# Memory's keys by 512-column products, and eight taps of a convolution moved to GpSimd, in a two-layer hybrid decoder

## What is computed

```python
z = rms_norm(x, mix_norm[l]) @ w_in[l]          # attention q, k, v; convolution; short convolution
ca, cg = jnp.split(zc, 2, axis=-1)
u = ca * jax.nn.sigmoid(cg)                     # 256 channels
u = causal_depthwise_conv(u, cc_dw[l]) + cc_dw_b[l]   # 31 taps for each channel
o_cc = jax.nn.silu(layer_norm(u, cc_ln_g[l], cc_ln_b[l]))
x = x + jnp.concatenate([o_att, o_cc, o_sc], axis=-1) @ w_out[l]
hq = (rms_norm(x, xa_norm[l]) @ xa_wq[l])       # cross attention, 4 heads of 256
kv = rms_norm(mem, mem_norm[l]) @ xa_wkv[l]     # 256 memory tokens: mk (keys), mv (values)
```

## Time and profile before

| | us |
|---|---|
| median of 3 runs | 1152.06 (1151.82 to 1153.53) |
| the profiled execution's own time | 1151.6 |
| its span in the trace | 1149.8 |
| granted TensorE clock | 0.999 of full |
| busy: PE, DVE, ACT, POOL | 1142.5, 845.7, 655.3, 24.0 |
| HBM traffic | 183 GB/s over the span |

### The profile page before, as it was taken

How to read it: one execution, slowest core, us unless ns; L and a number is a source line. 1 busy time by engine, 2 the same in 40 slices (tenths; PEclk the granted TensorE clock), 3 DMA queues, 4 the chain that set the end, 5 groups by cost and what they waited for, 6 DMA issues and landing times.

```text
span 1149.8 us, 15912 instructions
## 1 busy us (share of the span) xinstructions
PE 1142.5 (99%) x6316; PEld 993.5 (86%) x6316; DVE 845.7 (74%) x1152; ACT 655.3 (57%) x937; POOL 24.0 (2%) x63
## 2 busy tenths in 40 slices
PE   9999999999999999999999999999999999999997
PEld 8888888889889888888888888888898898888886
DVE  7767667899867676666776676669998676766756
ACT  6555656547755564545565554564577556645444
POOL 1000000001000000000000000000010000000000
PEclk9999999999999999999999999999999999999999
DMA  8965645643444366555546655544445443656551
GB/s 283 317 205 173 208 156 177 220 164 134 181 161 168 111 225 200 185 187 198 188 152 247 202 182 192 193 160 172 181 147 201 165 147 124 224 172 210 172 191 62
DMA packets 58970, 210.93 MB, mean 183 GB/s; under 512 B 4880, under 2 KB 15888, under 8 KB 52752
## 3 DMA queue, kind: packets, MB, share of 16 engines
q1 hardware_dynamic: 57920, 209.26, 53.7%
q10 hardware_dynamic: 976, 0.66, 0.2%
HBM read 208.85 MB, written 1.05 MB: 183 GB/s over the span
## 4 chain that ended last, share of the span: by engine, by line
PE 99%; DVE 0%; DVEq 0%; ACT 0%; issue 0%
PE G L1659 28%; PE G L1663 15%; PE D L1511 10%; PE D L1512 10%; PE D L1513 10%; PE G L1511 4%; PE G L1513 4%; PE G L1512 3%; PE G L1620 3%; PE G L1626 1%; PE D L1620 1%; PE D L1594 1%; PE D L1540 1%; PE D L1542 1%; PE D L1541 1%; PE G L1540 1%
## 5 line engine op out<-in xcount | busy, mean ns | idle before, releaser
L962 DVE TENSOR_TENSOR w_lo<-w_raw,w_hi 128x2048 fp32r<-128x2048 f32 (+3 forms) x260 | 452.5, 1747 | 58.4 <-ACT w_hi L556 57.2
L556 ACT ACTIVATE w_hi<-w_raw 128x2048 fp32r<-128x2048 f32 (+3 forms) x260 | 381.9, 1478 | 42.1 <-PE G L1513 18.4
L1659 PE MATMUL G<-a,w_hi 128*128 128x512 f32 x1406 | 339.8, 390 | 0.0
L1659 PEld LDWEIGHTS G<-a,w_hi 128*128 128x128 f32 x1406 | 260.8, 188 | 52.7 <-issue 0.9
L1663 PEld LDWEIGHTS G<-a,w_lo 128*128 128x128 f32 x1406 | 184.2, 191 | 9.5
L1663 PE MATMUL G<-a,w_lo 128*128 128x256 f32 x1406 | 187.0, 282 | 0.0
L1066 DVE TENSOR_TENSOR zqk<-G,zqk 128x512 f32<-128x512 f32 x88 | 60.8, 691 | 153.1 <-ACT zqk L635 152.8
L635 ACT ACTIVATE zqk<-G 128x512 f32<-128x512 f32 x88 | 52.5, 596 | 180.2 <-PE G L1663 180.0
L1511 PE MATMUL D<-w_hi,hT_hi 128*128 128x512 f32 x352 | 138.2, 393 | 0.0
L1512 PE MATMUL D<-w_lo,hT_hi 128*128 128x512 f32 x352 | 137.9, 392 | 0.0
L1513 PE MATMUL D<-w_hi,hT_lo 128*128 128x512 f32 x352 | 137.0, 389 | 0.0
(11 more groups left out here) (261 smaller groups left out, 1366.5 us busy)
## 6 DMA issues: line engine op xcount, KB each, us to landing
w_raw<-w_dram SPq DMA_DIRECT2D x128, 1024.0 KB, 5.1
w_raw<-w_dram SPq DMA_DIRECT2D x127, 512.0 KB, 5.5
m_raw<-memT_dram SPq DMA_DIRECT2D x2, 1024.0 KB, 10.1
w_raw<-w_dram SPq DMA_DIRECT2D x6, 256.0 KB, 5.6
w_raw<-w_dram SPq DMA_DIRECT2D x8, 128.0 KB, 3.8
vx<-mem_dram SPq DMA_DIRECT2D x1, 1024.0 KB, 11.8
x<-x_dram SPq DMA_DIRECT2D x2, 256.0 KB, 5.0
gbc<-fin_dram SPq DMA_DIRECT2D x1, 512.0 KB, 8.0
```

Of the source, the lines that this page charges most:

```text
L556: A(w_hi[:, part(i)], w_raw[:, part(i)], ACT.Copy).then_inc(s_hi, 1)
L962: V.tensor_tensor(w_lo[:, part(i)], w_raw[:, part(i)], w_hi[:, part(i)].bitcast(F32), ALU.subtract).then_inc(s_lo, 1)
L1659: M(banks[b], whi[:, at:at + P], both, start=k == 0, stop=False)
```

## The change

Blocks kv 0 to kv 3 are cut as 8 row groups of 256 columns and come in two transfers each. The memory's hi and lo are put in one tensor m, and `tall` is gone: the keys go through `head_queries` (renamed `head_columns`), 16 products of 512 columns and 16 of 256 for each block, with blocks alternating between DB[2:4] and G[0:2]. ACT and DVE make the keys' high and low parts after each of the four blocks, so TensorE waits for kvlo0 before kv 2, kvlo1 before kv 3, kvlo2 before kv 4, kvlo3 before kv 6, and for max1 already before kv 1. Taps 23 to 30 leave DVE; POOL computes them into acc3 (which is the tensor sig) as soon as u_pad is there, and DVE adds acc3 after acc2. The orders of ACT and DVE in the stretch kv 2 to kv 5 are rewritten.

```diff
+    name[1] == "kv" and name[2] < 4) else 1 for name, _ in RING_BLOCKS]
...
-        m_hi = sb("m_hi", [P, KD, T], F32R)
-        m_lo = sb("m_lo", [P, KD, T], F32R)
+        m = sb("m", [P, KD, 2, T], F32R)
+        m_hi, m_lo = m[:, :, 0, :], m[:, :, 1, :]
...
+        DVE_TAPS = 23
+        K_BANKS = (DD[:, 2:4, :], GG[:, 0:2, :])
...
+                pool.wait_ge(conv_act.sem, conv_act.at(l, "uT"))
+                for j in range(DVE_TAPS, KC):
+                    to = acc3 if j == DVE_TAPS else tap
+                    for c in range(2):
+                        last = nc.gpsimd.tensor_scalar(to[:, c, :], u_pad[:, c, j:j + T], col(C_CCW + c * KC + j), None,
+                                                       ALU.mult)
+                    if j > DVE_TAPS:
+                        pool.drain()
+                        last = nc.gpsimd.tensor_tensor(acc3[:, :, :], acc3[:, :, :], tap[:, :, :], ALU.add)
+                        if j < KC - 1:
+                            pool.drain()
+                last.then_inc(conv_pool.sem, conv_pool.one("taps"))
...
                 split(l, "kv", 2)
                 exp(0)
+                k_hi(0)
                 split(l, "kv", 3)
-                kv_hi(0)
+                k_hi(1)
                 aT_copy(0)
                 exp(1)
                 split(l, "kv", 4)
+                k_hi(2)
                 o_copy(0)
...
+                def kx_lo_part(i):
+                    dve.wait_ge(att_act.sem, att_act.at(l, f"kv{i}"))
+                    k = slice(2 * i, 2 * i + 2)
+                    V.tensor_tensor(kx_lo[:, k, :], K_BANKS[i % 2][:, :, 0:T], kx_hi[:, k, :].bitcast(F32), ALU.subtract)
+                    dve.drain()
+                    V.tensor_tensor(kx_lo[:, k, :], K_BANKS[i % 2][:, :, T:], kx_lo[:, k, :].bitcast(F32), ALU.add
+                                    ).then_inc(att_dve.sem, att_dve.one(f"kvlo{i}"))
...
                 split(l, "kv", 2)
+                kx_lo_part(0)
+                split(l, "kv", 3)
+                kx_lo_part(1)
                 scores(2)
-                taps(range(23, 25))
-                split(l, "kv", 3)
-                kv_lo(0)
                 combine(1)
-                taps(range(25, 27))
                 split(l, "kv", 4)
-                taps(range(27, 29))
+                kx_lo_part(2)
+                dve.drain()
+                V.tensor_tensor(acc[:, :, :], acc[:, :, :], acc2[:, :, :], ALU.add)
+                dve.drain()
+                dve.wait_ge(conv_pool.sem, conv_pool.at(l, "taps"))
+                V.tensor_tensor(acc[:, :, :], acc[:, :, :], acc3[:, :, :], ALU.add
+                                ).then_inc(conv_dve.sem, conv_dve.one("acc"))
                 split(l, "kv", 5)
-                kv_lo(1)
-                taps(range(29, 31))
...
+                    if i == 1:
+                        pe.wait_ge(att_dve.sem, att_dve.at(l, "max1"))
+                    if i in (2, 3, 4, 6):
+                        pe.wait_ge(att_dve.sem, att_dve.at(l, f"kvlo{(0, 0, 0, 1, 2, 0, 3)[i]}"))
...
+                    if i < 4:
+                        whi, wlo = weights(INDEX[l, "kv", i])
+                        head_columns(m, whi, wlo, (0, 1), (DB[2:4], G[0:2])[i % 2], range(KD), T).then_inc(s_blk, 1)
+                        return
```

More of the change, by code:

```diff
@@ L102 @@
 PLACE, BEFORE = ring_places()
-TRANSFERS = [2 if (name[1] == "q" and name[2] >= 4) or (name[1] == "in" and name[2] in (7, 8)) else 1 for name, _ in RING_BLOCKS]
+TRANSFERS = [2 if (name[1] == "q" and name[2] >= 4) or (name[1] == "in" and name[2] in (7, 8)) or (
+    name[1] == "kv" and name[2] < 4) else 1 for name, _ in RING_BLOCKS]
 def landed(i):
@@ L221, in hymba_kernel @@
         sq = sig
+        acc3 = sig
         std = sb("std", [P, T])
@@ L304, in hymba_kernel @@
         s_mlo = sem("mem_lo_ready")
+        conv_pool = signals("conv_pool", ["taps"])
         conv_pe = signals("conv_pe", ["uT", "sT", "gbT", "mean", "var"])
@@ L309, in hymba_kernel @@
         att_pe = signals("att_pe", "kT0 kT1 S0 S1 S2 aT0 pv0 aT1 pv1 aT2 pv2 oT0 oT1".split())
-        att_act = signals("att_act", ("q0 q1 k kT v elam exp0 kv0 aT0 exp1 o0 sso0 kv1 aT1 exp2 on0 kv2 aT2 o1 kv3 "
+        att_act = signals("att_act", ("q0 q1 k kT v elam exp0 kv0 kv1 aT0 exp1 kv2 o0 sso0 kv3 aT1 exp2 on0 kv4 aT2 o1 kv5 "
                                       "oT0 oT1").split())
-        att_dve = signals("att_dve", ("lam2 qlo0 qlo1 klo max0 max1 lam a0 max2 kvlo0 a1 kvlo1 a2 kvlo2 sso1 kvlo3 on1 "
+        att_dve = signals("att_dve", ("lam2 qlo0 qlo1 klo max0 max1 lam a0 kvlo0 kvlo1 max2 a1 kvlo2 kvlo3 a2 kvlo4 sso1 kvlo5 on1 "
                                       "oT0 oT1").split())
@@ L793, in o_copy, with k_hi, v_hi @@
                     last.then_inc(att_act.sem, att_act.one(f"o{t}"))
-                def kv_hi(ch):
+                def k_hi(i):
+                    act.wait_ge(s_blk, INDEX[l, "kv", 0] + i + 1)
+                    A(kx_hi[:, 2 * i:2 * i + 2, :], K_BANKS[i % 2][:, :, 0:T], ACT.Copy
+                      ).then_inc(att_act.sem, att_act.one(f"kv{i}"))
+                def v_hi(ch):
                     act.wait_ge(s_blk, INDEX[l, "kv", 0] + 2 * ch + 2)
                     for b in range(2):
[L799 to L804, removed]
+                        last = A(vx_hi[:, b, (ch - 2) * N:(ch - 1) * N], kv_banks(ch)[b][:, :], ACT.Copy,
+                                 scale=rmem[:, b:b + 1])
+                    last.then_inc(att_act.sem, att_act.one(f"kv{ch + 2}"))
                 split(l, "kv", 2)
                 exp(0)
+                k_hi(0)
                 split(l, "kv", 3)
-                kv_hi(0)
+                k_hi(1)
                 aT_copy(0)
@@ L1226, in mixer, with vx_lo_part @@
                 split(l, "kv", 1)
-                def kv_lo(ch):
-                    dve.wait_ge(att_act.sem, att_act.at(l, f"kv{ch}"))
-                    for b in range(2):
[L1232 to L1239, removed]
+                def kx_lo_part(i):
[5 more added lines that the diff above has]
+                                    ).then_inc(att_dve.sem, att_dve.one(f"kvlo{i}"))
+                def vx_lo_part(ch):
+                    dve.wait_ge(att_act.sem, att_act.at(l, f"kv{ch + 2}"))
+                    for b in range(2):
+                        w = slice((ch - 2) * N, (ch - 1) * N)
+                        last = V.scalar_tensor_tensor(vx_lo[:, b, w], kv_banks(ch)[b][:, :], rmem[:, b:b + 1],
+                                                      vx_hi[:, b, w].bitcast(F32), ALU.mult, ALU.subtract)
+                    last.then_inc(att_dve.sem, att_dve.one(f"kvlo{ch + 2}"))
                 def scores(g):
@@ L1317, in mixer @@
                                 ALU.subtract).then_inc(conv_dve.sem, conv_dve.one("acclo"))
+                combine(2)
                 split(l, "kv", 6)
@@ L1527, in wide @@
                 last.then_inc(s_blk, 1)
[L1529 to L1543, removed]
             def first_down(l, stage, i, hi, lo, ks, between):
@@ L1625, in head_queries @@
                         at = (k - ks[0]) * width + d * P
-                        last = M(banks[d][:, T:], wlo[:, at:at + P], a[:, k, 0, :], start=False, stop=k == KD - 1)
+                        last = M(banks[d][:, T:], wlo[:, at:at + P], src[:, k, 0, :], start=False, stop=k == KD - 1)
                 return last
@@ L1635, in first_queries @@
                     for h in range(2):
-                        last = head_queries(whi, wlo, (2 * h, 2 * h + 1), G, range(2 * i, 2 * i + 2), N, ready=8 * q)
+                        last = head_columns(a, whi, wlo, (2 * h, 2 * h + 1), G, range(2 * i, 2 * i + 2), N, ready=8 * q)
                         if (i, h) == (3, 0):
@@ L1643, in queries @@
                 whi, wlo = weights(INDEX[l, "q", 2 + h])
-                head_queries(whi, wlo, (0, 1), (DB[0:2], DB[2:4])[h - 2], range(KD), T, between=between).then_inc(s_blk, 1)
+                head_columns(a, whi, wlo, (0, 1), (DB[0:2], DB[2:4])[h - 2], range(KD), T, between=between).then_inc(s_blk, 1)
             def gate_up(l, f, c, ks, ready=None):
@@ L1875, in columns_free @@
                 def columns_free():
-                    pe.wait_ge(att_dve.sem, att_dve.at(l, "kvlo2"))
+                    pe.wait_ge(att_dve.sem, att_dve.at(l, "kvlo4"))
                 def o_transposes(t):
```

35 lines of the change are left out of this document (16 added, 19 removed).

## The result

The changed kernel takes 1160.99 us (median of 4 runs, 1160.68 to 1161.43), against 1151.94 us (1151.77 to 1153.53) for the kernel before, run beside it: a ratio of 1.0076, 95% interval 1.0058 to 1.0093. It is 9.1 us slower. 1158.0 us had been forecast, with a range of 1149.4 to 1165. The profiled execution took 1160.68 us, its span 1158.9; before, the span was 1149.8, so the spans differ by the same 9.1 us.

What follows compares the result with a forecast made beforehand. TensorE, busy 99% of the span, was taken to bound the kernel. 1151.6 less 1.4 of key-block gain plus 7.8 of stalls from POOL holding DVE gave 1158.0 us, range 1149.4 to 1165.

Steps and rivals of the forecast that it cites:

- TensorE's pace: Key blocks kv 0 to kv 3: 64 products fewer save 0.72 us a layer, 1.4 us for both.
- The late stretch and the transfers at 0: kv 1 to kv 6: new waits for the keys' low parts (tightest kvlo0, margin 0.5 us) and half-block transfers cost 0.
- Rival (b): Before kv 2: kvlo0 late, each layer stalls 0.5 us if the chain from S(0) comes 1 us later; 1151.2 us; chance 0.04.
- rival (c): POOL too slow, DVE waits for its taps: at 12 ns a column some 20 us a layer, 1190 us; chance 0.02.
- The mechanism: First part of mixer: POOL's SBUF reads hold DVE's taps and w_lo, 8.7 us, leaving 3.9 us stall a layer; chance 0.61.
- cost nothing: At 209.92, POOL's first four products run beside DVE's one-input first taps and add 0 us.
- POOL's time less 0.13: Hold of a DVE tap or w_lo: 0.36 - 0.13 = 0.23 us a product, 1.02 - 0.13 = 0.89 us a sum.
- The upper end of the range: 1165 us, where the two-tensor rate would be 2.4 ns a column and the one-input rate 1.8.
- Once TensorE has waited, all later margins are as before: After the stall at in 9, later waits keep their margins, so stall stays 3.9 us a layer, 7.8 in all.
- at in 9: TensorE stalls before in 9: 8.7 us of holds less 4.8 of DVE idle time and TensorE slack, 3.9 us a layer.
- the prediction's own mark: Right if TensorE stops 3 to 5 us before in 9; wrong if no gap there, or a gap at kv 2.
- Rival (a): DVE not held, or so little that its 4.8 us of cover takes it: only TensorE's gain, 1150.2 us; chance 0.33.

Runs made afterwards that it cites:

- the products alone: The changed kernel with POOL's 7 sums a layer replaced by pairs of memsets, its 16 products kept, taps 23 to 30 left out of the result: 1150.36 us.

## Why the prediction was right in sign and 3 us short

**TensorE's pace: right.** 0.72 us a layer was forecast, 0.70 measured.

**The late stretch and the transfers at 0: right.** kvlo0 is through in the changed kernel at 274.31 + 0.69 = 275.00, and kv 2 starts at 275.06. The margin went from the forecast 0.5 to next to nothing in the changed kernel, and was 0.43 with all taps on DVE. aT(0) to kv 2 takes 0.51 where it took 0.36, so at most 0.15 us of it is a wait. Rival (b) didn't come, but it was near. POOL's tensor was ready 39 us before DVE asked (247.68 against about 287), not 50; rival (c) is out.

**The mechanism: right for the sums, and for the products in part.** POOL and DVE delay each other where both read SBUF, DVE with two inputs. This is shown three ways: L1209 beside a sum takes 1.0 us more; DVE instructions with an input in PSUM are not touched; and with POOL's reads replaced by writes the taps are back at 480 ns. The other way round, a sum that starts within a w_lo takes 3.2 us where 1.29 is its own time, and a product 2.9 to 3.3 where 0.92 to 1.07 is. The rule of the Trainium skill, SBUF — State Buffer, section Who interferes with whom, is borne out for these: contention of two SBUF inputs with a GpSimd instruction that reads, and not with one that only writes. It says further that tensor_scalar can run in a mode that uses both ports and then contends as well. The 710 ns of the first taps beside memsets agree, against 412 without; which mode these instructions ran in, no row shows. What no run bears out is the exclusion for a whole instruction in the case of the products: they last 1 us and hold a tap by about a quarter of that at most, and there the measurement decides. The first four products, which were to "cost nothing" beside the one-input first taps, lengthen these by 0.47 us a layer.

**Sizes were off, and cancelled: that is luck.** A sum was put at 1.02 us with a hold of 0.89; it takes 1.29 and holds about 1.0. But seven holds were forecast, 6.2 us, and five came in the first layer, 5.1: the sum of 231.17 ran beside L1231 and L1233, which have an input in PSUM, and that of 219.68 ran mostly behind w_lo and beside gch, which has one too, and held the tap after them by 0.27. The estimate of 1.1 by the Trainium skill, GPSIMD Engine Reference, section 3.1, is 0.2 under the measured 1.29. A product was put at 0.36 us with a hold of 0.23; it takes 0.92 to 1.07 us undisturbed and yet holds a tap by only 0.05 to 0.25, 0.14 a product with the products alone. The estimate "POOL's time less 0.13" fits sums roughly (1.16 against 0.94 to 1.10) and not products. Why that is, no run shows. In all, DVE's instructions took 8.1 us more in the first layer and 8.4 in the second, where 8.7 was forecast. The upper end of the range has a slip: the rates named for it, 2.4 and 1.8 ns a column, give 1163.3 by the prediction's own sum, and not 1165; the measured time lies under both.

**The step that failed** is "Once TensorE has waited, all later margins are as before", and with it the stall "at in 9". The 8.7 of holds less the 2.1 of idle time leave DVE 6.6 us late. TensorE's wait at in 9 makes up only what goes beyond the 2.7 of slack there. The 2.7 themselves are used up: DVE stays 2.7 us nearer to TensorE than it was, and at klo there had been a margin of only 1.73. So the stall of a layer is DVE's lateness less the smallest margin up to the end of the holds, wherever it is: 6.6 - 1.73 = 4.9, and not 3.9. With this alone the forecast would have been 1151.6 - 1.4 + 9.7 = 1159.9 us, against a profiled 1160.68. The rest of the difference is the stalls of 4.85 and 5.25 where this has 4.85 twice, 0.3 behind the last product, and a gain of 1.33 and not 1.4. By the prediction's own mark (a stop of 3 to 5 us at in 9; wrong if there is none) the place was wrong: TensorE stops there for 0.12 us in the first layer and for 1.56 in the second, where one more sum had held a tap by then. For this there is a second cause: POOL's list is 38 us long and not 25, so nearly half of the holds of the first layer come behind that place.

**Rival (a)**, that DVE isn't held enough to matter, had a third of the chance. It is what happens with four taps on POOL (1151.69) and with the products alone (1150.36), and it would have been the case here if the holds had summed to less than the cover that four taps show, 1.7 + 1.73 = 3.4 us a layer, and not the 4.8 that the prediction counted.

## What to carry to other kernels

Work moved to an idle engine is not free if the two engines delay each other when both read SBUF, as POOL's sums and DVE's two-input instructions do here: the engine that was relieved may lose more than it gave away. Here eight taps, about 6.7 us of DVE a layer, came back as 8.1 to 8.4 us of longer DVE instructions, at a place where DVE mattered more. Then look for idle time on the first engine itself, whose places the profile names one by one; here they took three of the eight taps for nothing, and the late stretch had room for the other five. And when an engine falls behind over a long stretch, compare its lateness with the smallest margin of all waits in the stretch and behind it, up to where it next sits idle; a wait met earlier doesn't restore the margin that it used.

## What the runs showed of the hardware that was not expected

A POOL product of 256 columns with a scalar for each partition takes 0.92 to 1.07 us when undisturbed, and the sum of 512 columns 1.29. The product holds a DVE tap by 0.05 to 0.25 us, the sum by about 1.0. A POOL memset, which only writes, lengthens DVE's one-input tensor_scalar from 412 to 710 ns and leaves its two-input instructions alone (480 ns). And TensorE's granted clock fell to 0.53 for some 5 us behind a stall of 1.8 us in one profiled execution and not in another with as long a stall; what decides between the two stays open.
